# Where weights and moving operands stand in memory, and the order of a block's three products

## What is computed

```python
def reference(x, c, ...):
    x = first_block(x, c, w_ada, ...)
    return second_block(x, g_ffn1_2, w1_gate_2, ...)

# in first_block
mod = (c_act @ w_ada[i] + b_ada[i]).reshape(bsz, N_MOD, D_MODEL)[:, :, None, :]
u = rms_norm(x, ln1[i]) * (1.0 + scale1) + shift1
x = x + gate1 * mixer_sublayer(u, w_in[i], ...)
u2 = rms_norm(x, ln2[i]) * (1.0 + scale2) + shift2
hid = jnp.square(jax.nn.relu(u2 @ w_up[i]))
x = x + gate2 * (hid @ w_down[i])

# in second_block
x = x + 0.5 * swiglu(rmsnorm(x, g_ffn1[l]), w1_gate[l], w1_up[l], w1_down[l])
h = rmsnorm(x, g_mix[l])
p = h @ w_in[l]
x = x + jnp.concatenate([out_a, out_b], axis=-1) @ w_out[l]
x = x + 0.5 * swiglu(rmsnorm(x, g_ffn2[l]), w2_gate[l], w2_up[l], w2_down[l])
```

## The kernel before

| buffers | before | after |
|---|---|---|
| whi, wlo, raw, xT, ss, sq, rinv, ident, ones | 128 | 128 |
| ahi, alo, hhi, hlo, bhi, blo, clo, lhi, llo | 0 | 128 |
| xin, araw, braw, kF, qF, qaF, kaF, kiF, pT, va | 0 | 128 |
| chi, qc, bc, yhi, ylo, xwhi, xwlo | 64 | 128 |
| cv, xf, zs, xdt, xw, btok, seg, states | 64 | 128 |
| fraw, xg | 32 | 160 |
| score, tab64, qtok, vt, rl, biasM | 256 | 384 |

## Time and profile before

### The profile page before, as it was taken

How to read it: one execution, slowest core, us unless ns; L and a number is a source line. 1 busy time by engine, 2 the same in 40 slices (tenths; PEclk the granted TensorE clock), 3 DMA queues, 4 the chain that set the end, 5 groups by cost and what they waited for, 6 DMA issues and landing times.

```text
span 2287.7 us, 28544 instructions
## 1 busy us (share of the span) xinstructions
PE 2237.3 (98%) x10872; PEld 1829.0 (80%) x10872; DVE 1320.4 (58%) x1835; ACT 863.7 (38%) x1223; POOL 4.5 (0%) x8
## 2 busy tenths in 40 slices
PE   7999999999999999999999999999989899999998
PEld 5888888887888888888878888889868667888887
DVE  5577777777673475433475344355777766434344
ACT  5655555543222342322342222234445444212124
POOL 0000000000000000000000000000000000000000
PEclk9999999999999999999999999999999899999999
DMA  7323233224543243323222222223121002232321
GB/s 263 114 75 105 96 98 104 92 74 162 169 154 103 92 129 115 101 90 99 92 92 92 92 92 93 92 92 91 49 65 38 19 32 79 92 97 96 103 83 65
DMA packets 208140, 222.08 MB, mean 97 GB/s; under 512 B 9413, under 2 KB 200330, under 8 KB 205994
## 3 DMA queue, kind: packets, MB, share of 16 engines
q1 hardware_dynamic: 206362, 210.26, 28.5%
q10 hardware_dynamic: 1680, 10.49, 1.1%
HBM read 218.57 MB, written 2.16 MB: 96 GB/s over the span
## 4 chain that ended last, share of the span: by engine, by line
PE 87%; DVE 7%; ACT 3%; issue 2%; DMA 1%; ACTq 0%; DVEq 0%
PE G L551 24%; PE G L552 24%; PE G L553 24%; PE G L587 2%; PE G L589 2%; PE G L588 2%; DVE wlo L1806 1%; PE X L739 1%; ACT whi L1159 1%; PE G L1024 1%; DMA araw<-in_w_ada 1%; PE X L1041 1%; PE X L1007 1%; PE X L1031 1%; DVE score L2688 1%
## 5 line engine op out<-in xcount | busy, mean ns | idle before, releaser
L551 PE MATMUL G<-ahi,whi 128*128 128x512 f32 x1496 | 603.0, 403 | 4.1 <-DVE alo L2782 1.4
L552 PE MATMUL G<-alo,whi 128*128 128x512 f32 x1496 | 592.2, 396 | 0.0
L553 PE MATMUL G<-ahi,wlo 128*128 128x512 f32 x1496 | 591.9, 396 | 0.0
L1806 DVE TENSOR_TENSOR wlo<-raw,whi 128x2048 fp32r<-128x2048 f32 x176 | 403.3, 2292 | 240.2 <-ACT whi L1159 236.9
L1159 ACT ACTIVATE whi<-raw 128x2048 fp32r<-128x2048 f32 x176 | 335.5, 1907 | 454.9 <-PE G L553 434.3
L551 PEld LDWEIGHTS G<-ahi,whi 128*128 128x128 f32 x1496 | 282.9, 189 | 72.3 <-issue 2.4
L553 PEld LDWEIGHTS G<-ahi,wlo 128*128 128x128 f32 x1496 | 282.6, 189 | 67.2
L552 PEld LDWEIGHTS G<-alo,whi 128*128 128x128 f32 x1496 | 282.9, 189 | 66.7 <-issue 2.2
L551 PE MATMUL G<-hhi,whi 128*128 128x512 f32 x784 | 310.2, 396 | 0.7 <-DVE wlo L1806 0.7
L552 PE MATMUL G<-hlo,whi 128*128 128x512 f32 x784 | 309.6, 395 | 0.0
L553 PE MATMUL G<-hhi,wlo 128*128 128x512 f32 x784 | 309.5, 395 | 0.0
(11 more groups left out here) (410 smaller groups left out, 2783.6 us busy)
## 6 DMA issues: line engine op xcount, KB each, us to landing
raw<-in_w_in SPq DMA_DIRECT2D x43, 1024.0 KB, 5.1
raw<-in_w_up SPq DMA_DIRECT2D x38, 1024.0 KB, 5.3
raw<-in_w_down SPq DMA_DIRECT2D x32, 1024.0 KB, 5.1
raw<-in_w_gate SPq DMA_DIRECT2D x22, 1024.0 KB, 5.1
braw<-in_w_ada SPq DMA_DIRECT2D x12, 1024.0 KB, 5.1
raw<-in_w_in SPq DMA_DIRECT2D x20, 512.0 KB, 4.5
araw<-in_w_ada ACTq DMA_DIRECT2D x8, 1024.0 KB, 17.7
bc<-acum_dram SPq DMA_DIRECT2D x8, 1024.0 KB, 6.9
```

Source lines behind the costliest of these rows:

```text
L551: pe.matmul(bank[:], wh[:, j, f], rh[:, j, :], start=(j == 0), stop=False)
L552: pe.matmul(bank[:], wh[:, j, f], rl[:, j, :], start=False, stop=False)
L553: last = pe.matmul(bank[:], wl[:, j, f], rh[:, j, :], start=False, stop=(j == k - 1))
L1806: tt(wlo[s][:], raw[s][:], r32(whi[s][:]), ALU.subtract).then_inc(lo_split, 1)
```

## The change

A fixed buffer `to_weights` of 32 floats (128 bytes) goes in behind the fixed ones; `to_line`, 112 floats (448 bytes), behind `pre` in the scan's layout; and `PAD` grows from 12 to 124 floats, which the rounding makes 512 bytes where it was 64. In `fm_tile` the product with the low weights is issued second and that with the low activations third. No instruction is added or taken away on any engine.

```diff
@@ -60,7 +60,8 @@
 VECS, VROWS = 24, 77
-PAD = 12
+PAD = 124
+TO_WEIGHTS, TO_LINE = 32, 112
 HALVES = (slice(0, T // 2), slice(T // 2, T))
@@ -188,6 +189,7 @@
                 return [st.enter_context(nc.sbuf_tensor(s[0], s[1], s[2] if len(s) > 2 else F32)) for s in specs]
 
+        fixed("to_weights", [P, TO_WEIGHTS])
         split_a = (("ahi", [P, KB, T], F32R), ("alo", [P, KB, T], F32R))
@@ -200,8 +202,8 @@
-        (pacc, pre, cv, xf, zs, xdt, xw, btok, sm, seg, bc, states, yf, yhi, ylo, dts, dtw) = after_a(
-            "_s", ("pacc", [P, KB, T]), ("pre", [P, 4, 3 + T]), ("cv", [P, 4, T]), ("xf", [P, 4, T]),
+        (pacc, pre, _, cv, xf, zs, xdt, xw, btok, sm, seg, bc, states, yf, yhi, ylo, dts, dtw) = after_a(
+            "_s", ("pacc", [P, KB, T]), ("pre", [P, 4, 3 + T]), ("to_line", [P, TO_LINE]), ("cv", [P, 4, T]), ("xf", [P, 4, T]),
@@ -549,8 +551,8 @@
                     pe.matmul(bank[:], wh[:, j, f], rh[:, j, :], start=(j == 0), stop=False)
-                    pe.matmul(bank[:], wh[:, j, f], rl[:, j, :], start=False, stop=False)
-                    last = pe.matmul(bank[:], wl[:, j, f], rh[:, j, :], start=False, stop=(j == k - 1))
+                    pe.matmul(bank[:], wl[:, j, f], rh[:, j, :], start=False, stop=False)
+                    last = pe.matmul(bank[:], wh[:, j, f], rl[:, j, :], start=False, stop=(j == k - 1))
```

## The result

| | before | after |
|---|---|---|
| median | 2295.87 us (4 runs) | 2255.8 us (4 runs, 2252.24 to 2261.51) |
| ratio | | 0.9834, 95% interval 0.9812 to 0.9856 |
| span of the profiled execution | 2287.7 us | 2259.7 us |
| its mean granted clock | 0.993 | 0.984 |

A forecast was written before the change was run, and what follows sets the result against it. TensorE's step between 512-column products was taken to bound the kernel. Terms of -27.8 and -7.0 us took the 2287.7 us span to 2252.9, and 8.3 us around it gave 2261.2 us; range 2217 to 2332 us.

The forecast's parts named there:

- (1): 512-column products: moving operands come to the weights' place, step 232.6 to 228.9 ns over 7512 products, -27.8 us.
- (2): 256-column products: 1200 of them go from 119.1 to 113.3 ns, -7.0 us.
- nearness: 512-column products: chi's group, nearer the weights' place in two products of three, was taken as guide to 228.9 ns.
- (3): PAD and to_line: chi and clo might lose their gain, +0.4 us; the scan's full-precision products keep one place, 0 us.
- (4): Order of the three products: no product starts earlier or later, 0 us, bounds 2.5 us either way.
- (5): DMAs and other engines: landing places move from 0 to 128, VectorE and ScalarE read the same shapes, 0 us.
- the cover: Other engines' slack if TensorE steps faster: 12.6 us in a scan turn against 1.0 us needed; gain arrives in full.
- The sum's frame: Terms summed against the profiled span of 2287.7 us, with 8.3 us up to the median kept unchanged.
- The rule against it: Skill's rule of independent TensorE read ports: padding would do nothing, 2296 us; kept as a rival.
- Nothing: Rival: step locks at 233.3 to 233.5 ns wherever places are constant; 2296 to 2301 us, chance 0.22.
- Slower, since both streams start on the same piece of memory: Rival: moving stream and next weight load collide at equal places; steps at 237 ns, 2331.5 us, chance 0.25.
- Most of the excess goes: Rival: 512-column step falls to 218 ns, 2177 us, chance 0.08.

The follow-up runs named there:

- split_64_128: Changed kernel with hlo moved 64 bytes behind hhi's place and ylo 128 behind yhi's; mean steps 232.0 ns for h, 228.8 for y.
- order_only: Kernel before with the new order of the three products and the old pads; 2292.0 us against 2293.26, ratio 0.9998.
- pads_only: Changed kernel with the old order of the three products, so the pads alone; 2252.9 us, ratio 0.9825.
- all_at_0: Changed kernel with 96 floats of padding before raw, so weights and moving operands all stand at 0 modulo 512; span 2250.0 us.
- wlo_128: Changed kernel with the low weights alone moved 128 bytes off; span 2282.1 us, mean step of a products 231.2 ns.

## Why the prediction was right, and where its steps were off

Forecast 2261.2 us, measured 2255.8. The sign, the mechanism (places, not order) and the path (nothing else becomes late) were right. That the time came out within 6 us is partly luck: (1) put the gain 16.5 us too low and (2) 8 us too high, and the reason given for the size of (1) was wrong.

- **What bounds the kernel.** Right: the step of the 512-column products. The fastest 512-column group of before was the nearest row, and the step went beyond it. The 231.9 ns of the second stretch counts four products of one column among the others; the 512-column products there step 232.4, and the mean of all of them is 232.9, not 232.6, which is 2 us over 7512.
- **(1), the 512-column products.** The term that was mis-sized: -27.8 us forecast, with a step of 228.9; the step is 226.7 and the term -44.3 us. The step lies inside its bounds of 216 and 241. The reason that I gave for 228.9, nearness, was wrong: chi at a distance of 192 and clo at 128 are each slow alone (233.2 and 232.8), so neither place explains 228.9; what is left is that they alternate. No run tried that by itself, and in split_64_128 an alternation made the h products slower than either place alone. A distance of 32 is worse than one of 64.
- **(2), the 256-column products.** Wrong in sign: 120.0 ns instead of 119.1, about +1 us instead of -7.0. (The bound of 123 ns is worth +4.7 us, not +4.9.) xwhi's 113.3 was a good spell of an uneven run; over all of that group the mean step before was 116.2, and it is 119.8 now.
- **(3) and the scan.** The scan's full-precision products stayed as they were, mostly at 216 ns from record to record. I misread them, though: a turn of the scan issues three (x6 in the earlier trace rows), 24 in all where the group has 48, so each leaves two records and its 256 columns take 432 ns, four clocks a column and not two. They were a weaker guide to a step of 216 than I made of them. c gained 2 ns instead of losing any.
- **(4), the order.** 0 us, as forecast, by order_only (ratio 0.9998) and pads_only.
- **(5) and the cover.** VectorE's wait for the cast of weights is 234.2 us (236.9 in the earlier trace rows), ScalarE still idles 440.2 us before it (454.9), and raw's transfers take 5.1 us. Nothing else became late, as forecast.
- **The sum's frame.** I laid 8.3 us around the span. The profiled execution after took 2261.51 us with a span of 2259.7, so 1.8 us lie around it, as in every run whose span is on record; the rest of the 8.3 was that before's profiled execution was one of its quicker ones (its runs go from 2286.1 to 2298.3). And a term was missing: the lower clock in the second mixer, +11.2 us in the profiled execution. In all_at_0, with the same steps, that stage took 360.7 us instead of 368.4, with 24 us at the lower level instead of 41, so most of it is chance.
- **The rule against it.** By "PE and ACT never wait on anyone" (the Trainium skill, "SBUF — State Buffer", section "Who interferes with whom") the pads would have done nothing. The runs show that the rule, read as covering TensorE's own two reads, doesn't hold for these products: their step goes from 226.7 to 234.3 ns with the distance between the two operands.
- **Rivals.** "Nothing" fell with pads_only: y had stepped 233.5 at one constant place, and steps 226.5 at another. "Slower, since both streams start on the same piece of memory" fell: one place is the best of the ten distances tried. "Most of the excess goes" fell too: 13 of the 19 ns over the columns are still there.

## What to carry to other kernels

Where single-pass float32 products run back to back and each loads new weights, put the stationary and the moving operand at the same place modulo 256 bytes in their partitions, low parts included; that gave 6 ns of 233 a product, 1.7% of this kernel, for some hundred bytes of padding in each layout. For 256-column products there was nothing to gain. The pattern was measured with these shapes alone (128 stationary columns, 512 moving ones, slices that step by multiples of 512 bytes). Read the pace from counts of matmuls in a window in which TensorE never idles: its busy share was 98% before and after. A best row of a neighbouring group is a hint that something can be gained, not a model of why.

## What the runs showed of the hardware that I had not expected

The step depends on the distance of the two operands, and 256 bytes are as good as 0: 226.7 ns at both. Within 256 bytes it isn't smooth: 16, 32 and 64 bytes off give 231.7, 233.3 and 229.0 ns. At one place nearly all steps are 226 or 227 ns; at a distance of 128 the same instructions fall into one of two rhythms, a pair of 229 and 238 or a round of seven from 228 to 241, and keep to it for hundreds of microseconds. 256-column products don't share the gain: 119.8 ns at one place, 118.7 at 128, and 117.6 for the token products of wlo_128. And the same change can be seen as 28 or 37 us between two spans, by the executions of the changed kernel that one takes: 2259.7 us at a mean clock of 0.984, 2250.4 at 0.990, against 2287.7 before.
